# Finished retention rows go through HBM in 32-row blocks and are turned by VectorE, not by TensorE

## The chip, the cores and the metric

The kernel runs on one core of one Trainium2 chip. The metric is the time of one execution on the device in microseconds. Three executions of the kernel before gave a median of 1015.03 us (1014.83 to 1015.14).

## The reference, cut to what matters

The program is two blocks over a sequence of 256 tokens with 1024 features: two hybrid layers (attention and retention side by side, then an MLP) and after them two further mixers. The change lies in the hybrid layers, once in each of the two:

```python
def hybrid_layer(x, g_mix, w_in, sinks, w_a, w_b, w_out, g_mlp, w_up, w_down):
    h = rmsnorm(x, g_mix)
    z = h @ w_in
    aq, ak, av, rq, rk, rv, rg, ga, gb = jnp.split(z, SPLIT_POINTS, axis=-1)
    ...
    ya = sliding_window_sink_attention(aq, ak, av, sinks) @ w_a
    ...
    r = chunkwise_retention(rq, rk, rv)
    r = r * lax.rsqrt(jnp.mean(r * r, axis=-1, keepdims=True) + EPS)
    r = r.reshape(B, S, RET_V) * jax.nn.silu(rg.astype(jnp.float32))
    yb = r.astype(x.dtype) @ w_b
    mixed = jax.nn.sigmoid(ga) * ya + jax.nn.sigmoid(gb) * yb
    x = x + mixed @ w_out
    h2 = rmsnorm(x, g_mlp)
    return x + jnp.square(jax.nn.relu(h2 @ w_up)) @ w_down
```

Here r is 256 x 1024 and w_b is 1024 x 1024. Everything is float32.

## The kernel before, in words

The 256 tokens are two tiles of 128 (T = 2). All matmuls are float32 products made of three fp32r products: every operand is split into a rounded upper part and the remainder (w_hi and w_lo, hT_hi and hT_lo), and a product is hi*hi + hi*lo + lo*hi.

Weights come in pieces of 512 rows x 512 columns, 1 MB each, as a tile of 128 partitions x 4 row groups x 512 columns. SyncE (SP) issues all loads from one instruction stream, in the order of the pieces. A load waits until the piece four before it has been split, because it lands in that one's place. ScalarE (ACT) copies a landed piece to w_hi (line 1476) two pieces ahead of TensorE and VectorE (DVE) subtracts to get w_lo (line 1868). These two have a ring of three places: the split of piece p waits until TensorE has used piece p - 3.

Each engine's order of work is the order in which the code calls `step`, `window`, `gated` and so on; no planner is involved. In a layer the pieces are: twelve groups of w_in with two pieces each (RQ, RK, AQ, ... GB0, GB1), two pieces of w_a, four of w_b, four of w_out, then the MLP. `tokens_out` (TensorE) makes one group of 512 output columns for both token tiles; its result lies in the two banks OUT[0] and OUT[1], and its first matmul of a tile waits until the bank has been read (`out_ready`: `out_free[t]`).

Around the change the order is this. In the groups GB0 and GB1 `retention_out` (DVE, line 1972) writes the finished retention rows of tile 0 and of tile 1 to h, with tokens in the partitions, and counts r_ready. TensorE goes on with GB1 and with the two groups of w_a, USE_YA into OUT and USE_YA + 1 into banks 2 and 5. Then `turn_rows(h, ...)` (line 964) turns h by 16 transposes of 128x128 into four PSUM banks, so that features lie in the partitions; ACT copies the banks to hT_hi (`turn_hi`, line 1501) and DVE makes hT_lo (`turn_lo`, line 1884). With these TensorE makes the groups USE_YB and USE_YB + 1 from w_b.

The result of each w_a group is read by `gated` (DVE, line 2014), for tile 0 and tile 1. `out_free[t]` is counted by every `gated` in order, and the first matmul of USE_YB waits for a count that includes `gated` of USE_YA + 1 on its tile:

```python
n = l * USES + USE_YB          # tokens_out of the first w_b group
pe.wait_ge(out_free[t], n)     # out_ready: gated(0, ..., t) and gated(1, ..., t) are both done
```

One transfer of the same kind is there before: the rotated queries and keys of retention (z_ret) are stored to r_bounce in HBM (line 670, 1 MB), fetched back in four DMAs (line 675, one for each 32 partitions, 256 KB each), and turned in 32x32 blocks by one DVE instruction (line 2115).

Of the kernel before, what the change touches and what calls it, by code (L numbers as in the profile page):

```python
# [6 lines left out]
F32 = mybir.dt.float32  # L7
F32R = mybir.dt.float32r
ALU = mybir.AluOpType
# [152 lines left out]
def build_program(nc, ins, consts, where, out):  # L162
    ctx = ExitStack()
    with ctx:
# [3 lines left out]
        def sem(name):  # L168
            return ctx.enter_context(nc.semaphore(name))
# [91 lines left out]
        def area(start, *shape):  # L261
            n = int(np.prod(shape))
            assert start + n <= ARENA, (start, shape)
            v = arena[:, start:start + n]
            if len(shape) == 2:
                return v.rearrange("p (a b) -> p a b", a=shape[0])
            if len(shape) == 3:
                return v.rearrange("p (a b c) -> p a b c", a=shape[0], b=shape[1])
            return v
# [9 lines left out]
        rqT = area(13312, RET_HEADS, SEQ)  # L279
        rkT = area(14336, RET_HEADS, SEQ)  # L280
        rT = area(13312, 2 * RET_HEADS, SEQ)
        r_moved = area(5632, T * BLOCKS, 2 * RET_HEADS * BLOCK)
        r_bounce = nc.dram_tensor("r_bounce", [T * P, 2 * RET_HEADS * RET_QK], F32, kind="Internal").ap()
        s_far = area(15360, RET_HEADS * P)
# [111 lines left out]
        rot_done = [sem(f"rot_done{t}") for t in range(T)]  # L396
        rope_done = [sem(f"rope_done{t}") for t in range(T)]
        r_stored = sem("r_stored")
        r_blocks = sem("r_blocks")
        rT_ready = sem("rT_ready")  # L400
        att_turned = sem("att_turned")
# [114 lines left out]
        def square_piece(w, c, half):  # L516

            return w.rearrange("(k p) n -> p k n", p=P)[:, half * KP:half * KP + KP, c * COLS:(c + 1) * COLS]

        def last_piece(n):  # L520

# [95 lines left out]
        def _(sp):  # L617
# [26 lines left out]
            def load(piece):  # L644
# [17 lines left out]
                    sp.dma_start(raw_at(p)[:, :, 0:piece.shape[2]], piece).then_inc(raw_landed[RAW_SLOTS[p]], 16)  # L662
                n[0] += 1

            def blocks_moved(l, piece):

                if piece == 12:
                    for t in range(T):
                        sp.wait_ge(rot_done[t], l + 1)
                    sp.dma_start(r_bounce.rearrange("(t p) n -> p t n", p=P), z_ret).then_inc(r_stored, 16)  # L670
                if piece == 13:
                    sp.wait_ge(r_stored, 16 * (l + 1))
                    for b in range(BLOCKS):
                        at = slice(b * BLOCK, (b + 1) * BLOCK)
                        sp.dma_start(r_moved[at, :, :], r_bounce.rearrange("(u q) (b x) -> b q u x", q=BLOCK, b=BLOCKS)[b])\
                            .then_inc(r_blocks, 16)

            for l in range(DEPTH):
                for g in range(W_IN_GROUPS):
# [2 lines left out]
                        blocks_moved(l, 2 * g + half)  # L682
                for c in range(2):
                    load(square_piece(ins["w_a"][l], c, 0))
                for w in ("w_b", "w_out"):
                    for c in range(2):
                        for half in range(2):
                            load(square_piece(ins[w][l], c, half))
                for f in range(-2, F_GROUPS):
                    if l == DEPTH - 1 and f == 0:  # L690
                        for t in range(T):
# [58 lines left out]
        def _(pe):  # L750
# [463 lines left out]
            for l in range(DEPTH):  # L1214
# [6 lines left out]
                for g in range(W_IN_GROUPS):  # L1221
                    if l == 0 and g == 1:
                        second_group()
                    elif l or g:
# [4 lines left out]
                tokens_out(l * USES + USE_YA, l * PIECES + PIECE_A, 1, uT_hi, uT_lo)  # L1229
                tokens_out(l * USES + USE_YA + 1, l * PIECES + PIECE_A + 1, 1, uT_hi, uT_lo, banks=YA_BANKS,  # L1230
                           banks_free=lambda: pe.wait_ge(r_ready, 2 * l + 2))
                turn_rows(h, lambda t: r_ready, lambda t, i: 2 * l + t + 1)
                for c in range(2):
                    tokens_out(l * USES + USE_YB + c, l * PIECES + PIECE_B + 2 * c, 2, hT_hi, hT_lo,
                               turn=4 * l + 1 if c == 0 else None)
# [228 lines left out]
        def _(act):  # L1464
# [168 lines left out]
            for l in range(DEPTH):  # L1633
# [5 lines left out]
                for g in range(W_IN_GROUPS):  # L1639
# [4 lines left out]
                        step(p + 2 * g + 1)  # L1644
                    group_out(l, g)
                step(p + PIECE_A)
                step(p + PIECE_A + 1)
                turn_hi(4 * l + 1)
                for i in range(4):
                    step(p + PIECE_B + i)  # L1650
                turn_hi(4 * l + 2, scale=0.5)
# [206 lines left out]
        def _(dve):  # L1858
# [105 lines left out]
            def retention_out(l, t):  # L1964
# [8 lines left out]
                                                    in1=z_rg[:, t, at], op0=ALU.mult, op1=ALU.mult)  # L1973
                last.then_inc(r_ready, 1)

            def window(l, g):
                if g == 1:
                    dve.wait_ge(const_landed, 16)
# [112 lines left out]
            for l in range(DEPTH):  # L2091
# [12 lines left out]
                for g in range(W_IN_GROUPS):  # L2104
                    if g == 4:
                        window(l, g - 1)
                    if g != AKV and (l or g):
                        step(p + 2 * g)
                    if l == 0 and g == 1:
                        spread_dt()  # L2110
                    if g != 4:
                        window(l, g - 1)
                    if g == 5:
                        dve.wait_ge(r_blocks, 16 * BLOCKS * (l + 1))
                        dve.transpose(rT.rearrange("p s (u q) -> p u s q", q=BLOCK),
                                      r_moved.rearrange("p u (s f) -> p u s f", f=BLOCK)).then_inc(rT_ready, 1)
                    if g != AQ:
                        step(p + 2 * g + 1)
                    if g in (RG0, RG1):
                        for t in range(T):  # L2120
                            dve.wait_ge(tanh_ready, 4 * l + 2 * (g - RG0) + t + 1)
                            dve.scalar_tensor_tensor(out=z_rg[:, t, (g - RG0) * COLS:(g - RG0 + 1) * COLS], in0=rg_tanh[:, t, :],
                                                     scalar=1.0, in1=OUT[t], op0=ALU.add, op1=ALU.mult).then_inc(out_free[t], 1)
                for c in range(2):
                    step(p + PIECE_A + c)
                    for t in range(T):
                        gated(c, z_ga, l * USES + USE_YA + c, t, banks=(OUT, YA_BANKS)[c])
                turn_lo(4 * l + 1)
                for c in range(2):
                    step(p + PIECE_B + 2 * c)  # L2130
                    step(p + PIECE_B + 2 * c + 1)
# [532 lines left out]
```

## Time and profile before

| | |
|---|---|
| median of three runs | 1015.03 us |
| the profiled execution's own time | 1015.36 us |
| its span in the trace | 1013.4 us |
| TensorE busy (PE) | 1005.9 us, 99% |
| VectorE busy (DVE) | 719.7 us, 71% |
| ScalarE busy (ACT) | 504.4 us, 50% |
| GpSimd busy (POOL) | 170.3 us, 17% |
| granted TensorE clock | 0.999 |
| DMA, mean over the span | 183 GB/s |

The engines run side by side, so busy shares add up to more than the span. Times in the trace are counted from the start of the span; the profiled execution's own time is 1.96 us longer than the span. A row of the timeline has the start, the duration, the engine, the line, what is written and read, how many instructions it merges, and in brackets how long the engine was idle before and what ended that. "SPq" rows are DMAs issued by SyncE; a merged row's duration runs from the first issue to the end of the last. The time to landing of a DMA is counted from its issue.

### The profile page before, as it was taken

To read this page: it belongs to the slowest core of one execution; us is meant where nothing else is said; L and a number is where in the kernel's file an instruction comes from. 1 tells how busy PE (TensorE), PEld (TensorE's weight loads), DVE (VectorE), ACT (ScalarE), POOL (GpSimd) and SP (SyncE) were. 2 spreads that over 40 slices of the span, in tenths; PEclk is the share of its full clock that TensorE was granted. 3 is DMA by queue.
4 is the path that set the end of the run, shared out by engine and by line. 5 is a ranking of instruction groups with operands and counts; after the bars stand their busy time and mean duration, and the time that the engine had idled before them with its cause. 6 is when DMAs were issued, how large, how long until landed. Compare 5 with 4: busy or idle time off the path is not lost.

```text
span 1013.4 us, 13611 instructions
## 1 busy us (share of the span) xinstructions
PE 1005.9 (99%) x5677; PEld 851.7 (84%) x5677; DVE 719.7 (71%) x817; ACT 504.4 (50%) x620; POOL 170.3 (17%) x129
## 2 busy tenths in 40 slices
PE   9999999999999999999999999999999999999997
PEld 7888888888888888888788888888887899899796
DVE  5887746766565565797756667888877757789974
ACT  6545544454444545445554454444468545654352
POOL 0520010000000000430010020000000139159730
PEclk9999999999999999999999999999999999999999
DMA  9794455555555555594544557656654754355451
GB/s 337 252 306 128 163 166 166 169 175 196 193 184 206 166 176 178 186 293 164 166 150 142 168 147 279 197 185 208 199 175 135 233 182 166 125 166 145 116 188 42
DMA packets 100765, 185.47 MB, mean 183 GB/s; under 512 B 8840, under 2 KB 16096, under 8 KB 100576
## 3 DMA queue, kind: packets, MB, share of 16 engines
q1 hardware_dynamic: 100528, 184.51, 55.3%
q8 instruction: 45, 0.74, 0.3%
q10 hardware_dynamic: 176, 0.09, 0.0%
q14 instruction: 16, 0.13, 0.0%
HBM read 179.12 MB, written 3.15 MB: 180 GB/s over the span
## 4 chain that ended last, share of the span: by engine, by line
PE 99%; DMA 0%; DVE 0%; ACT 0%; SPq 0%; issue 0%; DVEq 0%; ACTq 0%
PE bank L766 14%; PE bank L768 12%; PE bank L769 12%; PE bank L1082 11%; PE bank L791 9%; PE bank L795 8%; PE bank L802 8%; PE bank L1086 6%; PE bank L1164 2%; PE bank L1388 1%; PE bank L964 1%; PE bank L948 1%; PE bank L773 1%; PE bank L783 1%; PE bank L1375 1%; PE bank L793 1%
## 5 line engine op out<-in xcount | busy, mean ns | idle before, releaser
L1868 DVE TENSOR_TENSOR w_lo<-arena,w_hi 128x2048 fp32r<-128x2048 f32 (+1 forms) x80 | 185.2, 2324 | 103.6 <-ACT w_hi L1476 103.3
L1868 DVE TENSOR_TENSOR w_lo<-raw,w_hi 128x2048 fp32r<-128x2048 f32 (+1 forms) x78 | 181.2, 2331 | 87.4 <-ACT w_hi L1476 87.2
L1476 ACT ACTIVATE w_hi<-raw 128x2048 fp32r<-128x2048 f32 (+1 forms) x83 | 157.1, 1893 | 100.3 <-PE bank L769 70.8
L1476 ACT ACTIVATE w_hi<-arena 128x2048 fp32r<-128x2048 f32 (+1 forms) x80 | 151.3, 1891 | 104.2 <-PE bank L769 80.4
L1082 PE MATMUL bank<-hT,w_hi 128*128 128x512 f32 x504 | 123.4, 391 | 0.0
L766 PE MATMUL bank<-w_hi,hT 128*128 128x512 f32 (+1 forms) x296 | 114.1, 386 | 0.0
L1082 PEld LDWEIGHTS bank<-hT,w_hi 128*128 128x128 f32 x504 | 92.2, 188 | 17.6
L2470 POOL TENSOR_TENSOR rstd<-mean,const 128x1 f32<-128x1 f32 (+1 forms) x16 | 9.1, 579 | 557.8 <-DVE mean L1877 388.5
L769 PE MATMUL bank<-w_hi,hT 128*128 128x512 f32 (+1 forms) x256 | 97.9, 382 | 0.0
L768 PE MATMUL bank<-w_lo,hT 128*128 128x512 f32 (+1 forms) x256 | 97.9, 382 | 0.0
L791 PE MATMUL bank<-w_hi,hT 128*128 128x512 f32 (+1 forms) x216 | 83.8, 391 | 0.0
L795 PE MATMUL bank<-w_hi,hT 128*128 128x512 f32 (+1 forms) x216 | 82.1, 382 | 0.0
L766 PE MATMUL bank<-w_hi,uT_hi 128*128 128x512 f32 x192 | 74.9, 390 | 0.0
L769 PE MATMUL bank<-w_hi,uT_lo 128*128 128x512 f32 x192 | 74.7, 389 | 0.0
L768 PE MATMUL bank<-w_lo,uT_hi 128*128 128x512 f32 x192 | 74.7, 389 | 0.0
L1086 PEld LDWEIGHTS bank<-hT,w_lo 128*128 128x128 f32 x504 | 67.0, 191 | 3.9
L1086 PE MATMUL bank<-hT,w_lo 128*128 128x256 f32 x504 | 68.3, 282 | 0.0
L766 PEld LDWEIGHTS bank<-w_hi,hT 128*128 128x128 f32 x296 | 55.6, 188 | 11.0
L791 PE MATMUL bank<-w_hi,uT_hi 128*128 128x512 f32 x160 | 62.5, 391 | 0.0
L795 PE MATMUL bank<-w_hi,uT_lo 128*128 128x512 f32 x160 | 62.5, 390 | 0.0
L802 PE MATMUL bank<-w_lo,hT 128*128 128x512 f32 (+1 forms) x216 | 56.1, 381 | 0.0
L769 PEld LDWEIGHTS bank<-w_hi,hT 128*128 128x128 f32 x256 | 48.1, 188 | 9.4
(347 smaller groups left out, 1891.0 us busy)
## 6 DMA issues: line engine op xcount, KB each, us to landing
arena<-in_w_in SPq DMA_DIRECT2D x22, 1024.0 KB, 5.2
raw<-in_w_in SPq DMA_DIRECT2D x20, 1024.0 KB, 5.7
arena<-in_w_up SPq DMA_DIRECT2D x16, 1024.0 KB, 5.8
raw<-in_w_up SPq DMA_DIRECT2D x16, 1024.0 KB, 5.3
arena<-in_w_down SPq DMA_DIRECT2D x16, 1024.0 KB, 5.2
raw<-in_w_down SPq DMA_DIRECT2D x16, 1024.0 KB, 5.2
raw<-in_e_w_in SPq DMA_DIRECT2D x6, 1024.0 KB, 5.2
arena<-in_e_w_in SPq DMA_DIRECT2D x6, 1024.0 KB, 5.2
```

The source lines that it names most:

```text
L766: pe.matmul(dst, a_hi, b_hi, start=first, stop=False, skip_group_check=shared)
L768: pe.matmul(dst, a_hi, b_lo, start=False, stop=False, skip_group_check=shared)
L769: mm = pe.matmul(dst, a_lo, b_hi, start=False, stop=last_one, skip_group_check=shared)
L773: pe.matmul(dst, a_hi, b_lo, start=False, stop=False, skip_group_check=shared)
L791: pe.matmul(dst, a_hi, b_hi, start=(start and i == 0), stop=False, skip_group_check=shared)
L795: pe.matmul(dst, a_lo, b_hi, start=False, stop=False, skip_group_check=shared)
L802: mm = pe.matmul(dst, a_hi, b_lo, start=False, stop=last_one, skip_group_check=shared)
L1082: pe.matmul(UP[j], w_hi[:, s[i], kk, at[j]], hT[:, k, :, :].rearrange("p e t -> p (e t)"), start=(i == kk == 0), stop=False, skip_group_ch ...
L1086: return pe.matmul(UP[j][:, 0:SEQ], w_lo[:, s[i], kk, at[j]], hT_hi[:, i * KP + kk, :], start=False, stop=(i == 1 and kk == KP - 1), skip_ ...
L1164: last = pe.matmul(OUT[t], a[:, KP * i + k, at[t]], w[:, s[i], k, :], start=(first and k == 0), stop=(last_one and k == KP - 1))
L1476: act.activation(w_hi[:, p % SPLIT_RING, :, 0:n], raw_at(p)[:, :, 0:n], copy).then_inc(hi_ready, 1)
L1868: dve.tensor_tensor(w_lo[:, s, :, 0:n], raw_at(p)[:, :, 0:n], w_hi[:, s, :, 0:n].bitcast(F32), ALU.subtract).then_inc(lo_ready, 1)
```

## The change

The 16 transposes on TensorE go, and with them the copies of ACT and DVE that read PSUM. In their place, for each token tile t:

- SP stores the finished rows of tile t, 128 x 1024, to h_bounce in HBM (`store_rows`, 512 KB), once r_ready says that they are there;
- when that has landed, SP fetches them back in four DMAs (`fetch_rows`, 128 KB each): DMA b takes the columns 256 b to 256 b + 255 to the partitions 32 b to 32 b + 31;
- DVE turns the tile's 32x32 blocks with one instruction over 128 x 1024 elements into h_raw (`turn_blocks` with across=True).

After both tiles ACT copies h_raw to hT_hi in four instructions and DVE subtracts four times to get hT_lo, all from SBUF. With this way of turning, slot k of partition p holds feature 8 p + k and no longer 128 k + p, so w_b's rows are loaded in the order "(p k)" in place of "(k p)" (`across_piece`).

```diff
@@ sync engine @@
+            def fetch_blocks(dst, src, done):
+
+                for b in range(BLOCKS):
+                    at = slice(b * BLOCK, (b + 1) * BLOCK)
+                    sp.dma_start(dst[at, :, :], src.rearrange("(u q) (b x) -> b q u x", q=BLOCK, b=BLOCKS)[b]).then_inc(done, 16)
...
+        def across_piece(w, c, half):
+
+            return w.rearrange("(p k) n -> p k n", p=P)[:, half * KP:half * KP + KP, c * COLS:(c + 1) * COLS]
...
-                for w in ("w_b", "w_out"):
-                    for c in range(2):
-                        for half in range(2):
-                            load(square_piece(ins[w][l], c, half))
+                def store_rows(t):
+
+                    sp.wait_ge(r_ready, 2 * l + t + 1)
+                    sp.dma_start(h_bounce[t * P:(t + 1) * P, :], h[:, t, :]).then_inc(h_stored[t], 16)
+
+                def fetch_rows(t):
+
+                    sp.wait_ge(h_stored[t], 16 * (l + 1))
+                    fetch_blocks(h_moved[:, t * BLOCKS:(t + 1) * BLOCKS, :], h_bounce[t * P:(t + 1) * P, :], h_blocks[t])
+
+                for c in range(2):
+                    for half in range(2):
+                        load(across_piece(ins["w_b"][l], c, half))
+                        if c == 0 and half == 1:
+                            store_rows(0)
+                        if c == 1 and half == 0:
+                            fetch_rows(0)
+                            store_rows(1)
+                            fetch_rows(1)
+                for c in range(2):
+                    for half in range(2):
+                        load(square_piece(ins["w_out"][l], c, half))
@@ tensor engine @@
-                turn_rows(h, lambda t: r_ready, lambda t, i: 2 * l + t + 1)
@@ scalar engine @@
                 step(p + PIECE_A)
+                act.wait_ge(piece_used, p + 2 * W_IN_GROUPS)
+                act.wait_ge(turned, 4 * (4 * l + 1) + 4)
+                for i in range(4):
+                    act.activation(hT_hi[:, 2 * i:2 * i + 2, :], h_raw[:, 2 * i:2 * i + 2, :], copy).then_inc(turned_hi, 1)
                 step(p + PIECE_A + 1)
-                turn_hi(4 * l + 1)
@@ vector engine @@
+            def turn_blocks(dst, src, slots, across=False):
+
+                rows_in = src.rearrange("p u (f s) -> p u s f" if across else "p u (s f) -> p u s f", s=slots)
+                return dve.transpose(dst.rearrange("p s (u q) -> p u s q", q=BLOCK), rows_in)
...
+                for t in range(T):
+                    dve.wait_ge(h_blocks[t], 16 * BLOCKS * (l + 1))
+                    last = turn_blocks(h_raw[:, :, t * P:(t + 1) * P], h_moved[:, t * BLOCKS:(t + 1) * BLOCKS, :], KD, across=True)
+                    if t == 0:
+                        order.link(last)
+                last.then_inc(turned, 4)
+                step(p + PIECE_A)
+                dve.wait_ge(piece_used, p + 2 * W_IN_GROUPS)
+                for i in range(4):
+                    dve.wait_ge(turned_hi, 4 * (4 * l + 1) + i + 1)
+                    dve.tensor_tensor(hT_lo[:, 2 * i:2 * i + 2, :], h_raw[:, 2 * i:2 * i + 2, :],
+                                      hT_hi[:, 2 * i:2 * i + 2, :].bitcast(F32), ALU.subtract).then_inc(turned_lo, 1)
                 for c in range(2):
-                    step(p + PIECE_A + c)
                     for t in range(T):
                         gated(c, z_ga, l * USES + USE_YA + c, t, banks=(OUT, YA_BANKS)[c])
-                turn_lo(4 * l + 1)
+                    if c == 0:
+                        step(p + PIECE_A + 1)
```

Line numbers differ between the two kernels, since the code has grown: the split on DVE is line 1868 before and 1900 now, `gated` is 2014 before and 2051 now, the loads are 662 before and 671 now.

VectorE between the last splits of w_a and the first ones of w_b in layer 0, before; w_lo rows are splits, the arena rows that read bank are `gated`, the hT rows are the lower parts:

```order
127 L1868 TENSOR_TENSOR w_lo<-raw,w_hi 128x2048 [waits hi_ready]
128 L1868 TENSOR_TENSOR w_lo<-arena,w_hi 128x2048 [waits hi_ready]
129 L2014 SCALAR_TENSOR_TENSOR arena<-arena,bank 128x512 [waits out0_done]
130 L2014 SCALAR_TENSOR_TENSOR arena<-arena,bank 128x512 [waits piece_used]
131 L1868 TENSOR_TENSOR w_lo<-arena,w_hi 128x2048 [waits hi_ready]
132 L2014 SCALAR_TENSOR_TENSOR arena<-arena,bank 128x512 [waits out0_done]
133 L2014 SCALAR_TENSOR_TENSOR arena<-arena,bank 128x512 [waits piece_used]
134 L1884 SCALAR_TENSOR_TENSOR hT<-bank,hT 128x256 [waits turned_hi]
```

The same place now; the transposes read the fetched blocks and write h_raw, both in arena:

```order
128 L2011 STREAM_TRANSPOSE arena<-arena 128x4x8x32 [waits h_blocks0]
129 L2011 STREAM_TRANSPOSE arena<-arena 128x4x8x32 [waits h_blocks1,dve_order]
130 L1900 TENSOR_TENSOR w_lo<-arena,w_hi 128x2048 [waits hi_ready]
131 L2170 TENSOR_TENSOR hT<-arena,hT 128x2x256 [waits turned_hi,piece_used]
132 L2170 TENSOR_TENSOR hT<-arena,hT 128x2x256 [waits turned_hi] x3
133 L2051 SCALAR_TENSOR_TENSOR arena<-arena,bank 128x512 [waits out0_done]
134 L2051 SCALAR_TENSOR_TENSOR arena<-arena,bank 128x512 [waits piece_used]
135 L1900 TENSOR_TENSOR w_lo<-arena,w_hi 128x2048 [waits hi_ready]
136 L2051 SCALAR_TENSOR_TENSOR arena<-arena,bank 128x512 [waits out0_done]
137 L2051 SCALAR_TENSOR_TENSOR arena<-arena,bank 128x512 [waits piece_used]
```

Two transposes and four subtractions stand ahead of all four `gated` instructions, where the lower parts stood behind them.

SyncE from the pieces of w_a on in layer 0, before:

```order
33 L662 DMA raw<-in_w_a 128x4x512 x2
34 L662 DMA arena<-in_w_b 128x4x512 x2
35 L662 DMA raw<-in_w_b 128x4x512 x2
36 L662 DMA arena<-in_w_out 128x4x512 x2
```

The same place now:

```order
33 L671 DMA raw<-in_w_a 128x4x512 x2
34 L671 DMA arena<-in_w_b 128x4x512 x2
35 L700 DMA h_bounce<-h_sb 128x1024
36 L671 DMA raw<-in_w_b 128x4x512
37 L678 DMA arena<-h_bounce 32x4x256 x4
38 L700 DMA h_bounce<-h_sb 128x1024
39 L678 DMA arena<-h_bounce 32x4x256 x4
40 L671 DMA raw<-in_w_b 128x4x512
41 L671 DMA arena<-in_w_out 128x4x512 x2
```

The third piece of w_b and the fetch of tile 0 stand between the two stores, and the fourth piece of w_b stands behind the fetch of tile 1.

ScalarE at the same place, before and then now, where the w_hi rows are splits:

```order
83 L1476 ACTIVATE w_hi<-arena 128x2048 x2
84 L1501 ACTIVATE hT<-bank 128x2x256 x4
85 L1476 ACTIVATE w_hi<-raw 128x2048 x2
```

```order
83 L1505 ACTIVATE w_hi<-arena 128x2048
84 L1679 ACTIVATE hT<-arena 128x2x256 x4
85 L1505 ACTIVATE w_hi<-arena 128x2048
86 L1505 ACTIVATE w_hi<-raw 128x2048 x2
```

The four copies to hT_hi have moved ahead of the split of w_b's second piece.

## Rows read from the trace of the kernel before

**Rows 1.** The page's first part: busy time of each engine

```profile
PE 1005.9 (99%) x5677; PEld 851.7 (84%) x5677; DVE 719.7 (71%) x817; ACT 504.4 (50%) x620; POOL 170.3 (17%) x129
```

**Rows 2.** The timeline of TensorE where the turns stand, in layer 0

```profile
165.91 1.91 PE L964 MATMUL bank<-const,h_sb 128*128 128x128 f32 x16
167.58 0.48 PE L766 MATMUL bank<-w_hi,hT 128*128 128x512 f32 x1
```

**Rows 3.** The same place in layer 1

```profile
551.58 0.48 PE L766 MATMUL bank<-w_hi,hT 128*128 128x512 f32 x1
```

**Rows 4.** The timeline of VectorE at this place, in layer 0

```profile
147.65 1.66 DVE L1972 SCALAR_TENSOR_TENSOR h_sb<-bank,ret_rstd,arena 128x256 f32<-128x256 f32 x4 [1.57 <-POOL ret_rstd L2591]
...
151.80 2.29 DVE L1868 TENSOR_TENSOR w_lo<-raw,w_hi 128x2048 fp32r<-128x2048 f32 x1 [2.49 <-ACT w_hi L1476]
157.75 2.29 DVE L1868 TENSOR_TENSOR w_lo<-arena,w_hi 128x2048 fp32r<-128x2048 f32 x1 [3.67 <-ACT w_hi L1476]
159.97 1.39 DVE L2014 SCALAR_TENSOR_TENSOR arena<-arena,bank 128x512 f32<-128x512 f32 x2
...
164.89 0.68 DVE L2014 SCALAR_TENSOR_TENSOR arena<-arena,bank 128x512 f32<-128x512 f32 x1
```

**Rows 5.** The timeline of SyncE: an earlier store, and pieces of w_b

```profile
47.14 0.37 SPq L662 DMA_DIRECT2D raw<-in_w_in  x1
48.34 0.37 SPq L670 DMA_DIRECT2D r_bounce<-arena  x1
...
55.70 1.83 SPq L675 DMA_DIRECT2D arena<-r_bounce  x4
...
138.74 0.37 SPq L662 DMA_DIRECT2D arena<-in_w_b  x1
...
144.69 9.79 SPq L662 DMA_DIRECT2D raw<-in_w_b  x2
```

**Rows 6.** DMA issues: name, count, size, median us from issue to landing

```profile
raw<-in_w_in SPq DMA_DIRECT2D x1, 1024.0 KB, 5.8
...
raw<-in_w_b SPq DMA_DIRECT2D x1, 1024.0 KB, 5.1
...
arena<-in_w_in SPq DMA_DIRECT2D x22, 1024.0 KB, 5.2
r_bounce<-arena SPq DMA_DIRECT2D x2, 1024.0 KB, 7.5
arena<-r_bounce SPq DMA_DIRECT2D x2, 256.0 KB, 6.3
...
out<-x_sb SPq DMA_DIRECT2D x3, 256.0 KB, 2.0
...
arena<-arena SPq DMA_DIRECT2D x1, 142.0 KB, 2.7
```

**Rows 7.** Windows: busy shares (instructions) of five engines, clock, DMA share, GB/s

```profile
59.00:60.00 1.00, 1.00 (x13) 1.00 (x11) 1.00 (x1) 1.00 (x2) 0.00 (x0) 1.00 1.15 193
```

**Rows 8.** Line 2115, the block turn of VectorE, with min/median/max ns

```profile
L2115 DVE STREAM_TRANSPOSE arena<-arena x2: 2302/2307/2312, 65.0 to 449.5; 128x2048 f32<-128x2048 f32 x2
```

**Rows 9.** The timeline of VectorE: a subtraction-sized instruction from SBUF and its follower

```profile
178.26 0.69 DVE L2137 TENSOR_TENSOR h_sb<-arena 128x512 f32<-128x512 f32 x1
178.87 0.68 DVE L2014 SCALAR_TENSOR_TENSOR arena<-arena,bank 128x512 f32<-128x512 f32 x1
```

**Rows 10.** The timeline of ScalarE at this place, in layer 0

```profile
155.82 1.91 ACT L1476 ACTIVATE w_hi<-arena 128x2048 fp32r<-128x2048 f32 x1
160.73 1.92 ACT L1476 ACTIVATE w_hi<-arena 128x2048 fp32r<-128x2048 f32 x1 [3.01 <-PE bank L769]
...
173.39 1.92 ACT L1476 ACTIVATE w_hi<-raw 128x2048 fp32r<-128x2048 f32 x1 [2.86 <-PE bank L769]
```

**Rows 11.** Windows at the end of the span, columns as in rows 7

```profile
1007.00:1008.00 1.00, 0.74 (x4) 0.28 (x2) 1.00 (x2) 0.22 (x1) 0.00 (x0) 1.00 0.00 0
...
1010.00:1011.00 1.00, 0.00 (x0) 0.00 (x0) 0.98 (x3) 0.00 (x0) 0.00 (x0) 0.97 0.00 0
```

More of the change, by code:

```diff
@@ L281, in build_program @@
         rT = area(13312, 2 * RET_HEADS, SEQ)
+        h_moved = area(0, T * BLOCKS, KD * BLOCK)
+        h_raw = area(13312, KD, SEQ)
+        h_bounce = nc.dram_tensor("h_bounce", [T * P, D], F32, kind="Internal").ap()
         r_moved = area(5632, T * BLOCKS, 2 * RET_HEADS * BLOCK)
@@ L398, in build_program @@
         r_stored = sem("r_stored")
+        h_stored = [sem(f"h_stored{t}") for t in range(T)]
+        h_blocks = [sem(f"h_blocks{t}") for t in range(T)]
         r_blocks = sem("r_blocks")
@@ L672, in blocks_moved @@
                     sp.wait_ge(r_stored, 16 * (l + 1))
[L673 to L676, printed above, removed]
+                    fetch_blocks(r_moved, r_bounce, r_blocks)
             for l in range(DEPTH):
@@ L2114, in _ @@
                         dve.wait_ge(r_blocks, 16 * BLOCKS * (l + 1))
-                        dve.transpose(rT.rearrange("p s (u q) -> p u s q", q=BLOCK),
-                                      r_moved.rearrange("p u (s f) -> p u s f", f=BLOCK)).then_inc(rT_ready, 1)
+                        turn_blocks(rT, r_moved, 2 * RET_HEADS).then_inc(rT_ready, 1)
                     if g != AQ:
```

## The prediction

> **What bounds the kernel now.** I read the busy times of the engines first: TensorE is busy 99% of the span, VectorE 71% [rows 1]. So what leaves TensorE's stream is gained in full, if nothing makes it wait instead. Then the timeline of TensorE around the 16 turns: the first starts at 165.91 and the first matmul of w_b at 167.58 [rows 2]. The stream has no hole there, since the rows of h have been ready since 149.31 (147.65 + 1.66 [rows 4]). Layer 1 repeats this 384.00 us later (551.58 against 167.58) [rows 2, 3]. The question is then whether the new way of the rows is done when TensorE gets to w_b. For this I read the timelines of VectorE, SyncE and ScalarE.
>
> **What TensorE saves.** 16 transposes hold the stream from 165.91 to 167.58, 1.67 us, in two layers 3.34 us. Nothing is added on TensorE.
>
> **What w_b's first matmul waits for now.** It needs h's upper parts, the split of w_b's first piece, and OUT[0] to have been read. The count for the last includes `gated` of the second w_a group on tile 0. Before, VectorE does this at 164.89 to 165.57 [rows 4], just ahead of 165.91. In the new order it stands behind the two block turns and four subtractions, and the second turn waits for the blocks of tile 1. So the end of the new path is: finished rows, store, fetch, and then VectorE's work down to that `gated`, in order.
>
> **Store of tile 1.** SyncE can issue it when the rows are ready, 149.31; it is behind the fetch of tile 0. The store of tile 0 is issued behind the second piece of w_b (138.74 [rows 5]), at 139.1. A store behind a 1 MB load, in the trace: the load is issued at 47.14 and lands 5.8 later, at 52.9; the store of 1 MB is issued at 48.34 and lands 7.5 later, at 55.8 [rows 5, 6], 2.9 behind the load. The 512 KB store of tile 0 then lands about half of this, 1.5, after the second piece (138.74 + 5.1 = 143.8), at 145.3. The third piece of w_b is issued at 144.69 and lands at 149.8 [rows 5, 6]. Fetch 0 is issued at 145.3 behind it, and moves its 512 KB when the piece is through, from about 149.2. Fetches that fill 32 partitions move 193 GB/s [rows 7], so 512 KB take 2.7 us, to 151.9. Store 1 is behind that and needs 1.5 more: it lands at 153.4 plus the latency of the end, for which I take 0.5: 153.9. From below: on idle queues 256 KB land 2.0 after issue [rows 6]; the 256 KB more cost 0.7 at the same rate as above (1.5 for 512 KB), so 152.0. From above: 154.5, if the end is as slow as with the earlier store. I take 153.9, since the trace shows DMAs of this queue landing one behind the other.
>
> **Fetch of tile 1.** Four issues take 1.83 us, 0.46 each [rows 5]. One 142 KB DMA on idle queues lands 2.7 after its issue [rows 6]. Below: last issue plus 2.7, 1.37 + 2.7 = 4.1. Above: first landing plus three times the data time of 128 KB (0.68 at 193 GB/s) plus 0.3 for their reading from HBM, 5.0. I take 4.55 between these. Issued at 153.9, the blocks are there at **158.45**; the bounds are 152.0 + 4.1 = 156.1 and 154.5 + 5.0 = 159.5. The four DMAs of the earlier fetch that were issued last landed after 6.3 (256 KB each, two of them, with a load ahead) [rows 6]; with such a tail it would be 160 to 161.
>
> **VectorE from there.** It is free since 154.09 (151.80 + 2.29 [rows 4]), so tile 0's turn is hidden. Then, from start to start:
> - turn of tile 1, 128x1024: half of 2.31 [rows 8], 1.15;
> - split of w_b's first piece: 159.97 - 157.75 = 2.22 [rows 4];
> - four subtractions of 128x512: 0.61 each (178.87 - 178.26 [rows 9]), 2.44;
> - two `gated`: 1.39 [rows 4];
> - split of the second piece: 2.2 again;
> - `gated` of the second group on tile 0: 0.68 [rows 4].
>
> That is 10.1 us. The read pattern of the turn steps by 8 elements, where the known one is contiguous; from below it costs nothing, from above I allow twice, 1.2 more. The subtractions wait for ScalarE's four copies: 128x2048 takes 1.92 [rows 10], so four quarters some 2.4 with their fixed parts, which end at 158.45 + 1.2 + 2.4 = 162.1; the fourth subtraction starts at 163.7. ScalarE's split of w_b's second piece stood at 160.73 [rows 10] and now follows the copies, 162.1 to 164.0; VectorE comes to it at 165.7. Both are hidden. With 0.05 for the signal, TensorE starts w_b at 158.45 + 10.1 + 0.05 = **168.6**. It stops at 165.91, so it idles 2.7 us, and is 1.02 later than the 167.58 of before.
>
> **What else changes, and costs nothing.** The fourth piece of w_b is issued behind fetch 1, at 155.8 instead of about 154.1, and lands by 161 to 163; ScalarE splits it at 173.39 [rows 10], so 10 us hide it, and the pieces of w_out behind it wait for splits as before. Reading w_b by "(p k)" sets a partition's rows 32 KB from the next one's; pieces of w_in, with rows of 5888 columns (23.5 KB apart), land in 5.2 and those of w_b in 5.1 [rows 6], so the pitch costs nothing, and at worst 1 us on the third piece, which would push the blocks of tile 1 by as much. ScalarE and VectorE no longer wait for turns in PSUM; behind w_b's start their order relative to TensorE is the old one, and the delay is not given back, since from there on TensorE has no holes to make it up in.
>
> **The sum.** Per layer +1.02, for two +2.0. In general the time changes by 2 x (blocks of tile 1 - 157.4), with the blocks' landing as above: break-even is at 157.4, and TensorE doesn't wait at all only before 155.8. The profiled execution took 1015.36 (span 1013.4 and 1.96 around it), so it would be 1017.4; against the median, 1015.03, it is 1017.1.
>
> **Rivals.**
> 1. *The round trip is short, and part of the gain stays.* The store finds the queues idle (152.0) or the fetch is at its lower bound, and the blocks are there at 156.1 to 156.5. TensorE then starts w_b at 166.25 to 166.65 and the time falls by 1.9 to 2.7, likeliest 1012.8. For it: both bounds are measured on idle queues, and little is moved between 149.8 and 154. Against it: it needs fetch 0 not to stand in front of store 1.
> 2. *All is hidden.* Blocks before 155.8: -3.34, 1011.7. It needs a round trip of 6.5 us from 149.31; the lower bounds give 6.8. Nearly excluded, unless the turns and subtractions are much faster than their rows.
> 3. *The wait eats just what is saved.* Blocks at 157 to 157.9, the time within 1 us of before, 1015.0. The forecast is only 0.5 to 1 us of landing away from it.
> 4. *A long tail, and the clock.* The last landing comes late as with the earlier fetch, at 160.5: TensorE idles 4.8 and the time rises by 6.2, 1021.2. At the end of the span TensorE stops in the slice from 1007 and its granted clock, 2.4 GHz until then, falls in the slice from 1010 (mean 0.97), that is after some 3.2 us without work [rows 11]. An idle time of 2.7 stays under this, one of 4.8 doesn't; each microsecond of matmuls at 1.2 GHz would then add half a microsecond, and with 2 to 4 of them per layer it is 2 to 4 more: up to 1025.
>
> The Trainium skill, "DMA: Bandwidth & Descriptors", in the section on the anatomy of one DMA, puts a DMA (from GpSimd's queue) at 2.0 us plus its bytes over 436 GB/s. The trace's idle-queue landings, 2.0 for 256 KB and 2.7 for 142 KB, lie on either side of the 2.6 and 2.3 of that rule. By it the store would take 3.2 and the last fetch 1.4 + 2.3, the blocks be there at about 156.3, and rival 1 be right: an estimate of 1012.8. It speaks of a DMA alone; what stands ahead in the queue is not in it, and the 7.5 of the earlier 1 MB store, 4.4 by the rule, shows how much that is.
>
> "VectorE: DVE Perf Modes", also in the Trainium skill, advises in its rules for kernel authors TensorE for a 128x128 transpose whose result may go to PSUM, which is against this change. Here TensorE pays 0.10 us for each turn, and the result has to be read by ScalarE and VectorE anyway.
>
> **How the numbers follow.** What a measurement of this kernel can tell from no change is about 0.2%, 2.0 us: below 1013.0 and above 1017.1. By the landing of the blocks: before 156.4 (rivals 1 and 2) 15%, of which 3% for rival 2; rival 3, 157.0 to 157.9, 17%, and what lies between it and rival 1 5%; the forecast, from 157.9 to 160, 51% (1016.0 to 1020.2, likeliest 1017.1); rival 4, 12%. The forecast's own range straddles the bound of 0.2%: 15 of its 51 lie within, 36 above. So: faster 15%, within 0.2% 37% (17 + 5 + 15), slower 48%. The range leaves out rival 2 with half of rival 1 below and the worse half of rival 4 above: 1012.8 to 1021.0.
>
> **What would show it.** The profile of the changed kernel should have no h rows among TensorE's transposes, and one wait per layer on TensorE's first matmul of w_b, on `gated` (VectorE), 2 to 4 us long. VectorE should idle before its second block turn, until the last landing of h_bounce at about 158.4, and then run its eleven instructions without a hole. Store 1 should land 4 to 5 us after its issue and not 2.7; each layer should be later by about 1 us at w_b. If TensorE's row of w_b follows that of w_a without a hole, the sum is wrong from the round trip on; if the hole ends with another wait (h's upper parts, or the split), VectorE's order is not what decides. If the hole is over 3.2 us, the granted clock behind it tells of rival 4.

## The result and the profile after

| | before | changed |
|---|---|---|
| median | 1014.96 us (1014.83 to 1015.14, 4 runs) | 1025.37 us (1024.50 to 1025.70, 4 runs) |
| ratio | | 1.0098 (95%: 1.0086 to 1.0111) |
| span of the profiled execution | 1013.4 us | 1023.9 us |
| PE / DVE / ACT busy | 1005.9 / 719.7 / 504.4 us | 1008.2 / 726.4 / 504.1 us |
| granted clock of the profiled execution, mean | 0.999 | 0.992 |

The change makes the kernel 10.4 us slower, against 2.1 forecast. The direction was right, the size was not, and the time lies outside the range. (The two medians divided give 1.0103, inside the interval of the ratio on record.) The other three executions of the changed kernel have a mean granted clock of 0.995 to 0.996 at 1024.50 to 1025.68 us, so how the excess divides between waiting and clock, below, is that of the profiled execution.

The longest of TensorE's waits in the changed kernel, the one that the kernel before doesn't have: engine, tile and line, what was waited for, us in total, times, longest.

```profile
PE bank L796 <- DVE w_lo L1900: 8.3, 2, 4.3
```

It comes once in each layer, as forecast; together that is 8.3 us. The row names the split that was last before the signal by the profile; the timeline of VectorE (below) shows that the `gated` behind it is what ends the wait. This is the timeline of TensorE, where [rows 2, 3] had 167.58 and 551.58 for the first matmul of w_b:

```profile
165.78 0.39 PE L799 MATMUL bank<-w_hi,uT_lo 128*128 128x512 f32 x1
170.14 0.76 PE L796 MATMUL bank<-w_hi,hT 128*128 128x512 f32 x1 [3.97 <-DVE w_lo L1900]
...
173.69 1.89 PE L813 MATMUL bank<-w_hi,hT 128*128 128x512 f32 x4
175.39 0.42 PE L796 MATMUL bank<-w_hi,hT 128*128 128x512 f32 x1
...
559.64 0.76 PE L796 MATMUL bank<-w_hi,hT 128*128 128x512 f32 x1 [4.34 <-DVE w_lo L1900]
...
564.73 0.39 PE L796 MATMUL bank<-w_hi,hT 128*128 128x512 f32 x1
```

w_b starts at 170.14, not at 168.6, and its first twelve matmuls take 5.25 us (170.14 to 175.39) and 5.09 (559.64 to 564.73). In the kernel before the same twelve took 2.83 (167.58 to 170.41). The reason is in the windows of this stretch, whose columns are those of [rows 7]:

```profile
167.00:168.00 1.00, 0.00 (x0) 0.00 (x0) 1.00 (x2) 1.00 (x1) 0.00 (x0) 1.00 1.04 406
168.00:169.00 1.00, 0.00 (x0) 0.00 (x0) 1.00 (x1) 0.17 (x1) 0.00 (x0) 0.80 0.05 18
169.00:170.00 1.00, 0.00 (x0) 0.00 (x0) 1.00 (x3) 0.00 (x0) 0.00 (x0) 0.50 0.00 0
174.00:175.00 1.00, 1.00 (x4) 0.71 (x4) 0.00 (x0) 0.00 (x0) 0.00 (x0) 0.50 0.56 133
175.00:176.00 1.00, 1.00 (x5) 0.81 (x4) 0.00 (x0) 0.00 (x0) 0.00 (x0) 0.79 1.04 391
```

The clock column (the last but two) falls from 1.00 (2.4 GHz) to 0.50 (1.2 GHz) in the slice from 168 and comes back in the slice from 175. The means of these two slices, 0.80 and 0.79, put the fall at 168.6 and the return at 175.4. TensorE's last matmul ended at 166.17, so the clock fell about 2.4 us later, and stayed low for 6.8 us, of which TensorE worked 5.3. Layer 1 is the same: 2.4 us after the last matmul, for 6.8 us.

The timeline of VectorE, which answers to [rows 4]:

```profile
147.74 1.66 DVE L2004 SCALAR_TENSOR_TENSOR h_sb<-bank,ret_rstd,arena 128x256 f32<-128x256 f32 x4 [1.57 <-POOL ret_rstd L2639]
...
154.10 2.15 DVE L2011 STREAM_TRANSPOSE arena<-arena 128x1024 f32<-128x1024 f32 x1
159.30 2.15 DVE L2011 STREAM_TRANSPOSE arena<-arena 128x1024 f32<-128x1024 f32 x1 [3.05 <-DMA arena<-h_bounce]
161.38 2.25 DVE L1900 TENSOR_TENSOR w_lo<-arena,w_hi 128x2048 fp32r<-128x2048 f32 x1
163.55 2.49 DVE L2170 TENSOR_TENSOR hT<-arena,hT 128x512 fp32r<-128x512 f32 x4
165.96 1.28 DVE L2051 SCALAR_TENSOR_TENSOR arena<-arena,bank 128x512 f32<-128x512 f32 x2
167.15 2.29 DVE L1900 TENSOR_TENSOR w_lo<-arena,w_hi 128x2048 fp32r<-128x2048 f32 x1
169.36 1.28 DVE L2051 SCALAR_TENSOR_TENSOR arena<-arena,bank 128x512 f32<-128x512 f32 x2
```

The order is the forecast one without a hole: turn, split, four subtractions, two `gated`, split, `gated`. The first of the last pair takes 0.68 of the row's 1.28 and ends at 170.04, and TensorE starts 0.10 later. The blocks were there at 159.30 (158.45 forecast). The turn takes 2.15 us for 128x1024, nearly the 2.31 that the known one takes for twice the elements [rows 8].

The timeline of SyncE, which answers to [rows 5], and the landings of the two stores and of the last fetch of layer 0:

```profile
139.25 0.50 SPq L700 DMA_DIRECT2D h_bounce<-h_sb  x1
144.79 0.37 SPq L671 DMA_DIRECT2D raw<-in_w_b  x1
146.37 2.12 SPq L678 DMA_DIRECT2D arena<-h_bounce  x4
149.43 0.34 SPq L700 DMA_DIRECT2D h_bounce<-h_sb  x1
154.49 1.73 SPq L678 DMA_DIRECT2D arena<-h_bounce  x4
```

```profile
h_bounce<-h_sb SPq DMA_DIRECT2D x1, 512.0 KB, 7.1
...
h_bounce<-h_sb SPq DMA_DIRECT2D x1, 512.0 KB, 5.0
...
arena<-h_bounce SPq DMA_DIRECT2D x1, 128.0 KB, 3.4
```

The store of tile 1 lands after 5.0 us (4.6 forecast, from 149.31 to 153.9), and the fetch's last DMA, issued at about 155.9, after 3.4, which is 4.8 from the first issue (4.55 forecast).

**The sum of the profiled execution.** Layer 0: w_b starts 2.56 later (170.14 against 167.58) and its twelve slow matmuls cost 2.42: 4.98. Layer 1: its start is 8.06 later than before, of which 4.98 are layer 0's, so 3.08, and the slow matmuls cost 2.26: 5.34. Together 10.3 of the 10.5 us between the spans.

### The profile page after: what moved, and what is told of

Same layout as the page of the kernel before. It is cut to its first block, busy times and chain, and to the rows that moved or that the text cites. A ratio compares the mean times of both kernels' runs of the same rounds, so it can differ in the third digit from the quotient of the medians.

```text
span 1023.9 us, 13569 instructions
## 1 busy us (share of the span) xinstructions
PE 1008.2 (98%) x5645; PEld 851.9 (83%) x5645; DVE 726.4 (71%) x813; ACT 504.1 (49%) x620; POOL 170.8 (17%) x129
## 4 chain that ended last, share of the span: by engine, by line
PE 91%; DMA 4%; DVE 3%; ACT 1%; issue 1%; SPq 1%; POOL 0%; DVEq 0%; ACTq 0%
PE bank L796 13%; PE bank L798 12%; PE bank L799 12%; PE bank L1112 11%; PE bank L821 8%; PE bank L825 7%; PE bank L832 7%; PE bank L1116 6%; PE bank L1194 2%; DMA raw<-in_w_in 2%; PE bank L1417 1%; PE bank L803 1%; PE bank L813 1%; DMA h_bounce<-h_sb 1%; PE bank L994 1%; PE bank L1404 1%
## 5 line engine op out<-in xcount | busy, mean ns | idle before, releaser
L796 PEld LDWEIGHTS bank<-w_hi,hT 128*128 128x128 f32 x296 | 56.9, 192 | 20.5 <-DVE w_lo L1900 9.1
L798 PEld LDWEIGHTS bank<-w_lo,hT 128*128 128x128 f32 x256 | 48.1, 188 | 9.4
```

The source lines that it names most:

```text
L796: pe.matmul(dst, a_hi, b_hi, start=first, stop=False, skip_group_check=shared)
L798: pe.matmul(dst, a_hi, b_lo, start=False, stop=False, skip_group_check=shared)
```

## The experiments

Theory A, after the result: VectorE's chain behind the last landing decides when w_b starts, the landing is late because the store stands behind other transfers, and in a hole of about 4 us the clock falls. Rival B: TensorE waits for the round trip, whatever VectorE does. Rival C: the slow clock costs little, or the new load order costs something. Rival D: a store to HBM is slow by itself. All ratios are against the kernel before on the same chip: e1 to e4 on one, with a median before of 1015.33, e5 to e8 on another, with 1015.35. The changed kernel's 1025.37 was taken beside a kernel before of 1014.96, so a difference between it and a row of this table carries some 0.4 us.

| | median us (range, runs) | ratio (95%) |
|---|---|---|
| e1 contiguous turn | 1022.02 (1019.98 to 1023.83, 4) | 1.0063 (1.0043 to 1.0082) |
| e2 28 spare matmuls | 1024.58 (1024.35 to 1025.26, 4) | 1.0088 (1.0071 to 1.0105) |
| e3 gated first | 1011.96 (1011.69 to 1012.95, 5) | 0.9966 (0.9953 to 0.9979) |
| e4 rows before third piece | 1018.21 (1015.64 to 1020.92, 10) | 1.0028 (1.0019 to 1.0038) |
| e5 load order alone | 1015.52 (1014.96 to 1015.91, 11) | 1.0000 (0.9991 to 1.0009) |
| e6 e1, e3 and e4 together | 1011.88 (1011.52 to 1012.07, 5) | 0.9963 (0.9949 to 0.9976) |
| e7 12 spare matmuls | 1021.08 (1020.33 to 1022.54, 4) | 1.0056 (1.0042 to 1.0069) |
| e8 no round trip | 1014.53 (1014.05 to 1015.25, 10) | 0.9991 (0.9982 to 1.0000) |

**e1: the turn reads contiguously**

```diff
-    last = dve.scalar_tensor_tensor(out=h[:, t, at], in0=src, ..., in1=z_rg[:, t, at], ...)
+    last = dve.scalar_tensor_tensor(out=h[:, t, at].rearrange("p (s f) -> p f s", s=KD),
+                                    in0=src.rearrange("p (f s) -> p f s", s=KD), ...)
...
-    turn_blocks(..., KD, across=True)
+    turn_blocks(..., KD)
```

> Changed kernel, but the rows of r are written in the order in which the block turn reads contiguously (the four writes of 128x256 per tile go out in steps of 32 elements); everything else as changed. Theory A (the hole before w_b is VectorE's chain after the last landing, and the clock falls in it): the second turn takes 1.2 us in place of 2.15, so w_b starts 0.95 earlier in each layer, the hole is 3.0 and 3.4 us and the clock still falls: 1023.4 us. If the clock stays up in one layer, 1021. Rival B (TensorE waits for the round trip through HBM whatever VectorE does): the hole stays above 4 us, 1025. If the stepped writes cost more than 0.2 us each, the store is issued later and up to half of the gain is lost.

The timeline of VectorE and, in the third row, of TensorE:

```profile
147.61 2.19 DVE L2004 SCALAR_TENSOR_TENSOR h_sb<-bank,ret_rstd,arena 128x256 f32<-128x256 f32 x4 [1.57 <-POOL ret_rstd L2640]
...
160.29 1.25 DVE L2012 STREAM_TRANSPOSE arena<-arena 128x1024 f32<-128x1024 f32 x1 [5.09 <-DMA arena<-h_bounce]
...
170.21 0.47 PE L796 MATMUL bank<-w_hi,hT 128*128 128x512 f32 x1 [4.18 <-DVE w_lo L1900]
```

The turn falls from 2.15 to 1.25 us: reading every eighth element is what made it long. The four stepped writes take 2.19 together in place of 1.66, 0.13 more each. In this profile of layer 0 the blocks came 1.0 us later than in the changed kernel, so the hole was as long as there (w_b at 170.21), and in layer 1 it was 4.03; the 3.0 and 3.4 that were expected did not come. The median is 3.3 below the changed kernel's, with runs in two groups: 1019.98 and 1020.32 at a mean granted clock of 0.999 and 0.997, and 1023.73 and 1023.83 at 0.994 and 0.996. The turn's share of the excess is shown by the row, 0.9 us per layer; the time of the whole kernel doesn't isolate it, since the hole decides the clock too. The windows show that:

```profile
169.00:170.00 1.00, 0.00 (x0) 0.00 (x0) 1.00 (x2) 0.00 (x0) 0.00 (x0) 1.00 0.00 0
170.00:171.00 1.00, 0.79 (x3) 0.69 (x4) 1.00 (x3) 0.00 (x0) 0.00 (x0) 0.84 0.30 33
```

With a hole of the same length the clock fell only in the slice from 170, after TensorE had started again, and came back in that from 174. It was low for 3.4 us there and again in layer 1, where it had 6.8 in the changed kernel, and w_b's first twelve matmuls took 4.42 and 4.16 us in place of 5.25 and 5.09. So the clock's cost for a hole of this length was 1.3 to 1.6 us here and 2.3 to 2.4 there.

**e2 and e7: spare matmuls in the hole**

```diff
+    keep_clock(3, 28)      # e7: keep_clock(3, 12)
     for c in range(2):
         tokens_out(l * USES + USE_YB + c, ...)
```

> Changed kernel, but 28 spare matmuls of 128x128 (about 2.9 us) into an unused bank fill the first part of the hole ahead of w_b in each layer. Theory A: w_b starts at the same moments as in the changed kernel (170.1 in layer 0), but at the full clock, which gives back 2.4 us per layer: 1020.5 us. Rival C (the low clock costs little, because the next pieces or VectorE set the pace there anyway): 1025 within 1 us. If the spare matmuls delayed w_b, it would be above 1025.

> Changed kernel with 12 spare matmuls in place of the 28 of e2: at the 0.23 us each that e2's trace showed they take 2.75 us and end at 168.8, before w_b can start at 170.1 or later. Theory A: the clock stays at its upper level over the hole and w_b's first twelve matmuls run in 2.8 in place of 5.25 us in layer 0: 1020.5 us (1019.5 to 1022 with the landing's scatter). Rival C (the low clock is hidden behind other work): 1025.

The timeline of TensorE in e2, with VectorE's second turn and last pair of `gated` in layer 0 between the layers:

```profile
166.05 6.41 PE L901 MATMUL bank<-const 128*128 128x128 f32 x56
172.93 0.47 PE L796 MATMUL bank<-w_hi,hT 128*128 128x512 f32 x1 [0.47 <-issue]
...
162.13 2.12 DVE L2012 STREAM_TRANSPOSE arena<-arena 128x1024 f32<-128x1024 f32 x1 [4.31 <-DMA arena<-h_bounce]
172.15 1.27 DVE L2052 SCALAR_TENSOR_TENSOR arena<-arena,bank 128x512 f32<-128x512 f32 x2
...
555.36 6.41 PE L901 MATMUL bank<-const 128*128 128x128 f32 x56
561.53 0.48 PE L796 MATMUL bank<-w_hi,hT 128*128 128x512 f32 x1
```

e2 missed, and by a fault of its design: a spare matmul (two rows of the trace each) takes 0.22 us, not the 0.10 of a transpose that I had counted. So 28 of them hold TensorE for 6.17 us from start to start (layer 1), where the transposes held it for 1.67: 4.5 more per layer, 9.0 in all, or 1024.3, and the runs gave 1024.35 to 1025.26. In layer 1 the filler holds up w_b by 1.0 us, since the `gated` that it needs had ended at 560.46. In layer 0 it doesn't decide: the blocks landed 2.8 us later than in the changed kernel (162.13 against 159.30), that `gated` ended at 172.83, and w_b started 0.10 behind it; why the landing was late is open. The clock did stay up (1.00 in every slice), which gave back about what the filler cost. In e7 the filler fits:

```profile
165.85 2.84 PE L901 MATMUL bank<-const 128*128 128x128 f32 x24
170.35 0.47 PE L796 MATMUL bank<-w_hi,hT 128*128 128x512 f32 x1 [1.66 <-DVE w_lo L1901]
172.27 1.07 PE L813 MATMUL bank<-w_hi,hT 128*128 128x512 f32 x4
```

w_b starts at 170.35, as late as in the changed kernel, but its ninth matmul comes 1.92 us later and not 3.55 (170.14 to 173.69). The median is 1021.08, 4.3 below the changed kernel, or 4.7 if each is counted from the kernel before beside it (5.7 against 10.4). This is the clock's part, 2.1 to 2.3 us per layer, in line with the 2.42 and 2.26 of the rows, and rival C's slow clock that costs little falls.

**e3: VectorE reads the banks of w_a first**

VectorE's order, in words (`-` changed kernel, `+` e3):

```diff
-    turn tile 0; turn tile 1; step(PIECE_A)
-    four subtractions
-    gated(0, ..., 0); gated(0, ..., 1); step(PIECE_A + 1); gated(1, ..., 0); gated(1, ..., 1)
+    turn tile 0; step(PIECE_A); turn tile 1
+    gated(0, ..., 0); gated(0, ..., 1); two subtractions; gated(1, ..., 0)
+    two subtractions; gated(1, ..., 1); step(PIECE_A + 1)
```

> Changed kernel, but VectorE's order around the second turn is another: turn of tile 0, split of w_b's first piece, turn of tile 1, both gated of the first w_a group, two subtractions, gated of the second group on tile 0, two subtractions, gated on tile 1, split of w_b's second piece. Theory A: OUT[0] is free at about 165.3 in layer 0, the blocks (159.3) and ScalarE's copies are in time, so TensorE has no hole and the clock stays: the 3.3 us of the transposes are gained, 1011.7 us. Rival B (the round trip itself is what is waited for): the wait only changes its name and the hole stays at 2 us or more, 1018 to 1025.

The timeline of VectorE and then that of TensorE:

```profile
157.85 2.29 DVE L1900 TENSOR_TENSOR w_lo<-arena,w_hi 128x2048 fp32r<-128x2048 f32 x1 [1.60 <-ACT w_hi L1505]
160.06 2.12 DVE L2011 STREAM_TRANSPOSE arena<-arena 128x1024 f32<-128x1024 f32 x1
162.09 1.24 DVE L2051 SCALAR_TENSOR_TENSOR arena<-arena,bank 128x512 f32<-128x512 f32 x2
163.25 1.28 DVE L2168 TENSOR_TENSOR hT<-arena,hT 128x512 fp32r<-128x512 f32 x2
164.46 0.68 DVE L2051 SCALAR_TENSOR_TENSOR arena<-arena,bank 128x512 f32<-128x512 f32 x1
...
165.78 0.39 PE L799 MATMUL bank<-w_hi,uT_lo 128*128 128x512 f32 x1
166.00 0.39 PE L796 MATMUL bank<-w_hi,hT 128*128 128x512 f32 x1
```

The `gated` that TensorE needs is done at 165.14, and w_b starts at 166.00, 0.22 after the start of w_a's last matmul, as one matmul follows another, without a hole. The time is 1011.96, 3.4 below before: the whole price of the transposes. The round trip is as long as in the changed kernel (the fetch is issued at 154.69) and costs nothing: VectorE makes the first split while it runs, the second split has gone behind the last `gated`, and the `gated` that TensorE needs has only two of the four subtractions ahead. Rival B falls. e3 moves these three together, and no run moves one alone. An estimate from the changed kernel's rows: the four subtractions alone, moved behind that `gated`, would take 2.4 us out of a hole of 4.0.

**e8: the changed order without the round trip**

```diff
-    store_rows(0) ... fetch_rows(0); store_rows(1); fetch_rows(1)
-    turn_blocks(h_raw[...], h_moved[...], KD, across=True)
+    turn_blocks(h_raw[...], h[:, t, :].rearrange("p (u x) -> p u x", u=BLOCKS), KD, across=True)
```

> Changed kernel without the stores and fetches: VectorE turns the blocks straight from h as soon as the rows are ready, in the order of the changed kernel. Left out is the move of blocks between partitions, so the values that enter w_b are wrong. Theory A: the second turn ends at 158.4 and the rest of VectorE's chain (8.7 us) puts w_b's start at 167.2, a hole of 1.2 us: 1014.5 us, so of the 10.4 us only the part above this is the round trip's, and VectorE's order alone uses up most of what the transposes gave. Rival B (the round trip is all there is to it): 1011.7.

Left out is the move of the blocks between partitions; VectorE's work is the same.

```profile
153.97 4.45 DVE L2007 STREAM_TRANSPOSE arena<-h_sb 128x1024 f32<-128x1024 f32 x2
...
167.08 0.47 PE L792 MATMUL bank<-w_hi,hT 128*128 128x512 f32 x1 [1.05 <-DVE w_lo L1896]
```

Even without the stores and fetches there is a hole of 1.05 us, and the time is 1014.53, as expected, 0.8 below before. So of the 3.4 us that the transposes were worth, the changed order of VectorE and its stepped turns use up 2.6 (1014.53 against e3's 1011.96); the round trip and the clock that falls in its hole add the other 10.8 (1025.37 against 1014.53). It is not the order by itself, as the expectation has it: the two turns, back to back here, take 4.35 us from start to start. At the 1.17 of e1 each they would end 2.0 earlier, and there would be no hole (an estimate; no run has both).

**e4: both stores and fetches ahead of the third piece of w_b**

```diff
                         if c == 0 and half == 1:
                             store_rows(0)
-                        if c == 1 and half == 0:
                             fetch_rows(0)
                             store_rows(1)
                             fetch_rows(1)
```

> Changed kernel, but SyncE issues both stores and both fetches ahead of the third piece of w_b; VectorE's order as changed. Theory A with transfers in the order of the queue: fetch of tile 0 is through before the store of tile 1 is issued, which lands in about 2.7 in place of 5.0 us; the blocks of tile 1 are there 2.3 us earlier, w_b starts at 167.9 in layer 0 and the hole is 2.0 us, too short for the clock to fall: 1016 us. If the clock falls all the same, 1020. Rival D (the store's 5.0 us are its own, writing to HBM is slow): landing and hole as in the changed kernel, 1025.

Landings of the store of tile 0 in layer 0 and of the store of tile 1 in layer 1, and TensorE's first matmul of w_b in each layer:

```profile
h_bounce<-h_sb SPq DMA_DIRECT2D x1, 512.0 KB, 8.4
...
h_bounce<-h_sb SPq DMA_DIRECT2D x1, 512.0 KB, 2.6
```

```profile
169.62 0.47 PE L795 MATMUL bank<-w_hi,hT 128*128 128x512 f32 x1 [3.03 <-DVE w_lo L1899]
...
553.66 0.47 PE L795 MATMUL bank<-w_hi,hT 128*128 128x512 f32 x1 [1.41 <-DVE w_lo L1899]
```

In layer 1 the store of tile 1 has no load ahead of it, only the end of tile 0's fetch (its last DMA landed at about 537, the store was issued at 535.52), and it lands after 2.6 us, so rival D falls; that the 5.0 of the changed kernel come from what stands ahead is the reading left. There the blocks were ready 7.3 us after the rows (542.83 against 535.49), against 10.3 in the changed kernel's layer 1. In layer 0 the store of tile 0 took 8.4 behind a load, its fetch was issued only at 148.13, and the store of tile 1 was behind it again and took 3.7. The clock was 0.999 over this profiled execution, with holes of 3.0 and 1.4. The ten runs scatter over 5 us, where the runs before scatter over 1.4: the median of 1018.21 is above the 1016 expected. The profiled execution, at 1017.5, had a late landing in layer 0. The mean granted clock is 0.997 to 0.999 in nine of the ten runs, as in those of the kernel before (0.998 to 1.000), and 0.995 in the slowest, at 1020.92: it will have fallen there, though no trace of that run shows it, but most of the scatter is in how long the transfers take. Why they vary is open.

**e5: the kernel before with the new load order of w_b alone**

```diff
-    load(square_piece(ins["w_b"][l], c, half))
+    load(across_piece(ins["w_b"][l], c, half))
...
-    pe.transpose(..., src[:, t, k * P:(k + 1) * P], ident)
+    pe.transpose(..., src[:, t, :].rearrange("p (j k) -> p k j", k=KD)[:, k, :], ident)
```

> Kernel before, with only w_b's rows loaded in the new order; TensorE's transposes of h read columns k, k + 8, k + 16, ... so that the result is the same. Theory A: the load order costs nothing, 0 +- 0.5 us against before, and a 1 MB piece of w_b still lands in 5.1 us. Rival C (rows 32 KB apart load slowly): the pieces land a microsecond or more later, though 10 us of lead hide it. If the stepped reading of the transposes costs, it shows as more than 1.67 us between the last matmul of w_a and the first of w_b.

```profile
165.51 1.95 PE L969 MATMUL bank<-const,h_sb 128*128 128x128 f32 x16
167.21 0.48 PE L770 MATMUL bank<-w_hi,hT 128*128 128x512 f32 x1
```

The ratio is 1.0000 (0.9991 to 1.0009), w_b's pieces of layer 0 land after 5.1 to 5.3 us (5.0 and 5.1 before), and the transposes hold TensorE for 1.70 in place of 1.67. The load order is free.

**e6: e1, e3 and e4 together**

> VectorE's order of e3, the contiguous block turn of e1 and SyncE's order of e4 in one kernel. Theory A: e3 already leaves no hole on TensorE, so the other two can only add slack: the same 3.3 us below before as e3, within 0.7 us; the spread of the runs should be no wider than that of before. Rival B (the landing still decides in some runs): faster than e3 by more than 0.7 us.

```profile
163.60 0.68 DVE L2051 SCALAR_TENSOR_TENSOR arena<-arena,bank 128x512 f32<-128x512 f32 x1
```

It is as fast as e3 (1011.88 against 1011.96), with a spread of 0.55 us; the `gated` that matters ends at 164.28, 0.9 earlier than in e3, which is slack and not time. Both beat the kernel before and the changed one.

## Why the prediction missed

- **The transposes' price, 1.67 us per layer: right.** e3 and e6 gain 3.4 us, which is all of it and no more.
- **What w_b waits for: right.** OUT[0], read by the `gated` at the end of VectorE's new chain; the rows of the changed kernel show the forecast sequence, and e3 removes the hole by this order alone.
- **The landing of tile 1's blocks, 158.45 forecast: 0.85 late in layer 0**, inside its bounds of 156.1 to 159.5, and 0.4 later still in layer 1, counted from the rows. From the rows on, the round trip took 9.9 (149.40 to 159.30) and 10.3 us (538.53 to 548.82), where 9.1 was forecast. The order of transfers was as argued; the store of tile 0 took 7.1 us behind its load, not 6.2, and pushed what stood behind it.
- **The block turn, 1.15 forecast: 2.08 from start to start.** This is the first term that was mis-sized. I had allowed up to 1.2 more for the stepped reading, but put the sum at the lower end. e1 shows the reading is the cause: 1.25 without it.
- **The rest of VectorE's chain, 9.0 forecast: 8.76** (161.38 to 170.14).
- **The clock: this is the step that failed.** "An idle time of 2.7 stays under this" rested on one row at the end of the span, where the clock fell 3.2 us after the last matmul [rows 11], taken as a bound. In the changed kernel it fell after 2.4 us, in both layers. The sum put the clock at nothing, and it went to rival 4 with a chance of 12%. Yet a landing 0.85 late and a turn 0.93 longer were both inside the bounds I had given, and together stretched the 2.7 us of idle time to 4.1 in layer 0 (170.14 against 166.01, when the next matmul could have started) and 4.5 in layer 1. What the clock then cost is 4.7 us: 2.42 and 2.26 by the rows, 4.3 to 4.7 by e7. Without it the time would have been 1020.7, still above the forecast but inside the range. Rival 4's time, with the clock, was up to 1025, and that is what happened, with its reason only in part: it wanted the blocks at 160.5, and counted 2 to 4 us of matmuls at the low clock per layer where there were some 5.

Put back into the prediction's own formula, 2 x (landing - 157.4), the measured landing and the turn give 2 x (159.30 + 0.93 - 157.4) = 5.7 us. e7, with the clock held up, measures 5.7 above before on its chip (1021.08 against 1015.35). That the two agree to 0.1 is in part luck: the rest of the chain was 0.24 shorter than in the formula, and layer 1's landing later. The remaining 4.3 to 4.7 of the 10.4 are the clock.

The rule of the Trainium skill that the prediction weighed ("DMA: Bandwidth & Descriptors", the anatomy of one DMA: 2.0 us plus the bytes over 436 GB/s) gives 3.2 us for the store. The runs lie on both sides of it: 2.6 in e4's layer 1, with only the end of a fetch ahead, and 5.0 in the changed kernel behind a load and a fetch. The rule has no term for what stands ahead, and here that was worth more than its distance from 2.6.

The error under the turn and the clock was to take each term at its middle or low end and then ask of the middle case alone whether the clock falls. The hole's length is the sum of all terms, and the cost rose by another 2.3 to 2.4 us per layer where it got long: the chances should have been taken over the sum.

## What to carry to other kernels

When work moves from the bounding engine to another, look for what the other engine does for the bound one further down its own queue: here another order of the same instructions, with one split ahead of the wait, the other split and two subtractions behind the read of the PSUM bank that TensorE waited for, turned +10.4 us into -3.4. A wait in front of an in-order engine's queue should have only that work behind it that needs the waited-for data. And where the bounds of a forecast, added up, allow a longer hole on TensorE than its middle does, price the clock too: holes of 4.0 to 4.3 us cost another 1.3 to 2.4 us each here, those of 3.0 and less nothing.

## What the runs showed of the hardware

- The granted clock's fall did not come at one fixed time after the last matmul. It came 2.4 us after it in both layers of the changed kernel, and 4.7 and 5.3 us after it in e1, when TensorE was at work again. The holes, by the profile's count, were 3.97 and 4.34 us in the one and 4.18 and 4.03 in the other. The clock was then low for 6.8 us each time in the changed kernel and for 3.4 in e1. In the hole of 3.03 in e4 it did not fall at all. In e7 1.66 us of idle time behind 2.84 of spare matmuls left it up.
- The block turn of VectorE in fp32 takes 1.25 us for 128x1024 read contiguously and 2.15 read with a step of eight elements (32 bytes). Writes with a step of 32 elements cost an instruction of 128x256 0.13 us more.
- A store of 512 KB lands after 2.6 us with only the end of a fetch ahead (e4, layer 1), after 5.0 behind a load and a fetch, and after 7.1 to 8.5 when it is issued 0.4 us behind a 1 MB load.
- A full fp32 matmul of 128x128 takes 0.22 us from start to start (28 of them 6.17 in e2), where a transpose of the same size takes 0.10.
